# Retention layer: the prompt's inner products and state from rounded high and low parts, norm weights loaded head by head

## The reference, cut to what matters

```
def step(s, inp):
    qi, ki, vi = inp
    scores = jnp.einsum('bhik,bhjk->bhij', qi, ki) * decay_mat
    inner = jnp.einsum('bhij,bhjv->bhiv', scores, vi)
    cross = jnp.einsum('bhik,bhkv->bhiv', qi * q_decay, s)
    s_new = chunk_decay * s + jnp.einsum('bhjk,bhjv->bhkv', ki * k_decay, vi)
    return s_new, inner + cross
```

## Time and profile before

| what | value |
|---|---|
| time, median of 3 executions | 662.84 us (662.42 to 663.81) |
| the profiled execution, its span from first to last instruction | 663.5 us |
| what the page gives around the span | nothing; the slowest of the timed executions is 663.81 us |
| PE busy | 619.0 us, 93% of the span |
| DVE busy | 373.7 us, 56% |
| ACT busy | 231.5 us, 35% |
| POOL busy | 223.6 us, 34% |
| mean granted clock of PE | 0.978 |
| norm weights, one transfer | 1024 KB, 10.2 us to landing |

### The profile page before, as it was taken

The page is one execution under the profiler, slowest core; times in us unless marked ns, Lnnn a source line. Parts: engine busy times, 40 slices in busy tenths (PEclk is TensorE's granted clock), DMA queues, the critical chain, the costliest instruction groups (busy, mean ns, idle before and its releaser), DMA issues. The chain is left out here.

```text
span 663.5 us, 11322 instructions
## 1 busy us (share of the span) xinstructions
PE 619.0 (93%) x4307; PEld 383.2 (58%) x4307; DVE 373.7 (56%) x718; ACT 231.5 (35%) x475; POOL 223.6 (34%) x239
## 2 busy tenths in 40 slices
PE   6999999999999999998999999999999988659996
PEld 5676647664766476643467756677744555344441
DVE  3343847474747474726553733345797974783822
ACT  4255232623262326214142615555134246231010
POOL 0060218021802180214075248999910012020000
PEclk9899999999999999998999999999999999798998
DMA  8997376777687769794796563454999999999982
GB/s 297 379 389 283 127 254 218 285 289 254 221 302 271 251 215 325 257 382 186 279 329 233 200 203 126 146 194 131 392 368 406 410 408 405 410 399 409 401 349 87
DMA packets 82193, 190.28 MB, mean 287 GB/s; under 512 B 4119, under 2 KB 12583, under 8 KB 82012
## 3 DMA queue, kind: packets, MB, share of 16 engines
q1 hardware_dynamic: 80484, 183.70, 74.9%
q0 software_dynamic: 1120, 4.46, 1.9%
q10 hardware_dynamic: 536, 1.41, 0.6%
HBM read 167.14 MB, written 22.41 MB: 286 GB/s over the span
## 5 line engine op out<-in xcount | busy, mean ns | idle before, releaser
L533 POOL TENSOR_TENSOR weights_low<-ring,weights_high 128x512 fp32r<-128x512 f32 x96 | 123.9, 1330 | 81.4 <-PE bank L780 45.3
L1360 ACT ACTIVATE weights_high<-ring 128x1024 fp32r<-128x1024 f32 x84 | 86.6, 1055 | 103.7 <-PE bank L799 75.5
L791 PE MATMUL bank<-weights_high,h_high 128*128 128x512 f32 x272 | 109.2, 401 | 0.0
L791 PE MATMUL bank<-weights_high,h_low 128*128 128x512 f32 x272 | 106.9, 393 | 0.0
L799 PE MATMUL bank<-weights_low,h_high 128*128 128x512 f32 x272 | 82.5, 401 | 1.2 <-DVE weights_low L533 0.9
L791 PEld LDWEIGHTS bank<-weights_high,h_high 128*128 128x128 f32 x272 | 51.1, 188 | 25.5 <-issue 14.3
L533 DVE TENSOR_TENSOR weights_low<-ring,weights_high 128x512 fp32r<-128x512 f32 x72 | 44.8, 687 | 28.3 <-PE bank L780 16.9
L799 PEld LDWEIGHTS bank<-weights_low,h_high 128*128 128x128 f32 x272 | 49.9, 188 | 14.9 <-DVE weights_low L533 3.9
L791 PEld LDWEIGHTS bank<-weights_high,h_low 128*128 128x128 f32 x272 | 51.1, 188 | 11.1
L1675 POOL TENSOR_TENSOR keys_by_sequence<-key_parts,consts 128x2048 fp32r<-128x2048 f32 x4 | 15.1, 3764 | 111.0 <-DVE key_parts L1973 111.0
L1939 DVE SCALAR_TENSOR_TENSOR ring<-ring,bank 128x512 f32<-128x512 f32 x64 | 41.8, 685 | 17.8 <-PE bank L971 16.9
(11 more groups left out here) (257 smaller groups left out, 1011.8 us busy)
## 6 DMA issues: line engine op xcount, KB each, us to landing
ring<-in_w_ada SPq DMA_DIRECT2D x12, 2048.0 KB, 13.5
ring<-in_cache_k SPq DMA_DIRECT2D x40, 512.0 KB, 8.7
ring<-in_cache_v SPq DMA_DIRECT2D x40, 512.0 KB, 10.0
ring<-in_w_ret_in SPq DMA_DIRECT2D x8, 2048.0 KB, 11.4
ring<-in_state_ret SPq DMA_DIRECT2D x32, 512.0 KB, 9.5
out_state_sample<-ring SPq DMA_DIRECT2D x32, 512.0 KB, 6.1
ring<-in_w_moba_in SPq DMA_DIRECT2D x8, 2048.0 KB, 9.0
arena<-in_cache_k SPq DMA_DIRECT2D x24, 512.0 KB, 10.9
```

What stands on the lines that cost most here:

```text
L533: tensor_tensor(w_low[:, slot, k, :], ring[:, slot, k * CH:(k + 1) * CH], high[:, k, :].bitcast(F32), ALU.subtract).then_inc(low_ready[LOW ...
L791: pe.matmul(o[i][:, :], xs[p][i][:, k, :], high[:, k, :], start=k == 0 and p == 0, stop=False)
L1360: nc.scalar.activation(w_high[u[0] == "moba"][:, 2 * i:2 * i + 2, :].rearrange("p a b -> p (a b)"), w[:, 2 * i * CH:(2 * i + 2) * CH], ACT ...
```

## The change

The prompt's output rows and its state are no longer plain fp32 products. Values, decayed keys and decayed scores are split: ACT writes a rounded high part, DVE the low part, and PE adds three rounded products (high times high, low times high, high times low) for each plain one. One wait of PE is added, on `kd_ready`. `v_low`, `kd_low` and `s_low` take the places of `v`, `kd` and the scores; the high parts have places of their own. The norm weights are now loaded one head at a time by POOL, after the gate products of the head before, and POOL waits for them ahead of the gate products.

PE:

```
-                sealed(pe.matmul(o[:, :], L0["sT"][:, 0, :], v[:, 0, :], start=True, stop=True), ...)
+                def by_parts(o, pairs):
+                    terms = [(x, y) for high, low, v_n in pairs
+                             for x, y in ((high, v_high[:, v_n, :]), (low, v_high[:, v_n, :]), (high, v_low[:, v_n, :]))]
+                    for i, (x, y) in enumerate(terms):
+                        last = pe.matmul(o[:, :], x, y, start=i == 0, stop=i == len(terms) - 1)
+                    return last
+                sealed(by_parts(o, [(s_high[:, 0, :], s_low[:, 0, :], 0)]), ("row", "o", h, 0))
...
+                sealed(by_parts(o, [(s_high[:, 1, :], s_low[:, 1, :], 1), (s_high[:, 2, :], s_low[:, 2, :], 0)]),
+                       ("row", "o", h, 1))
...
-                        last = pe.matmul(o[:, :], kd[:, n, j * P:(j + 1) * P], v[:, n, :], start=n == 0, stop=n == 1)
+                    pe.wait_ge(kd_ready, 2 * h + 2)
+                    sealed(by_parts(o, [(kd_high[:, n, js], kd_low[:, n, js], n) for n in range(2)]), ("S", h, j))
```

ACT (the copy to `kd` now writes `kd_high`):

```
                 high_weights(("ret", h, 2), range(2, 4))
+                for n in range(2):
+                    o = wait_full(act, ("row", "ret", h, 1, n))
+                    nc.scalar.activation(v_high[:, n, :], o[:, :], ACT.Copy).then_inc(v_high_ready, 1)
                 if h:
                     for n in range(3):
                         turned(L0["yT"][:, 4 * h - 4:4 * h, :], ("yT", h - 1, n), n)
...
                 copy_part(("ada", 1, ADA_FIRST[h]))
+                act.wait_ge(s_plain_ready, h + 1)
+                nc.scalar.activation(s_high..., s_plain, ACT.Copy).then_inc(s_high_ready, 1)
```

DVE (the three value copies ahead of the `qkT` copies are gone; behind them now stands):

```
+                for n in range(2):
+                    wait_read(dve, ("row", "ret", h, 0, n))
+                    nc.vector.scalar_tensor_tensor(kd_low[:, n, :], L0["k"][:, n, :], const("kdec_n")...,
+                                                   kd_high[:, n, :].bitcast(F32), ALU.mult, ALU.subtract).then_inc(kd_ready, 1)
+                    o = wait_full(dve, ("row", "ret", h, 1, n))
+                    dve.wait_ge(v_high_ready, 2 * h + n + 1)
+                    read_out(nc.vector.tensor_tensor(v_low[:, n, :], o[:, :], v_high[:, n, :].bitcast(F32),
+                                                     ALU.subtract), label)
+                o = wait_full(dve, ("row", "ret", h, 1, 2))
+                read_out(nc.vector.tensor_copy(v[:, 2, :], o[:, :]), label)
                 low_weights(dve, nc.vector.tensor_tensor, ("ret", h, 2), ...)
...
+                wait_read(dve, ("scores", h))
+                dve.sem_inc(s_plain_ready, 1)
                 modulation_turned(1, ADA_FIRST[h])
+                dve.wait_ge(s_high_ready, h + 1)
+                nc.vector.tensor_tensor(s_low..., s_plain, s_high..., ALU.subtract).then_inc(sT_ready, 1)
```

POOL:

```
-            pool.dma_start(L0["gn"], t["ret_gn_g"].rearrange("o h v -> o (h v)").partition_broadcast(P)
-                           ).then_inc(gn_in, 16)
+            pool.dma_start(L0["gn"], t["ret_gn_g"][:, 0, :].partition_broadcast(P)).then_inc(gn_in, 16)
...
+                pool.wait_ge(gn_in, 16 * (h + 1))
                 for n in range(3):
                     ...
+                if h + 1 < RH:
+                    pool.wait_ge(gate_ready, 3 * h + 3)
+                    pool.dma_start(L0["gn"], t["ret_gn_g"][:, h + 1, :].partition_broadcast(P)).then_inc(gn_in, 16)
```

More of the change, by code:

```diff
@@ L81, in const_table @@
     put("kdec_0", gamma[None, :] ** (2 * P - 1.0 - i[:, None]) * DK ** -0.5)
+    put("kdec_n", np.concatenate([gamma[None, :] ** (n * P - 1.0 - i[:, None]) for n in (2, 1)], 1))
     put("cdec", gamma[None, :] ** (P - 1.0 - i[:, None]))
@@ L335, in build @@
                  ("qkT", (3, 4, P)), ("qpad", (2, NS * (32 + TS))),
-                 ("sT", (2, P)), ("sTc", (P,)), ("sTs", (32,)), ("S1", (2, DV)), ("yT", (RET_VT, ROWS)), ("gn", (RH * DV,))]
+                 ("sT", (2, P)), ("sTc", (P,)), ("sTs", (32,)), ("S1", (2, DV)), ("yT", (RET_VT, ROWS)), ("gn", (DV,)),
+                 ("vh", (2, DV)), ("kdh", (2, DK)), ("sTh", (3, P))]
         spec1 = [("slots", (2, KT * CH)), ("G", (3, D)), ("qbT", (MH * 4, 32)), ("qd", (2, D)), ("v", (3, D)),
@@ L369, in build @@
         vmix = rounded("value_parts", (DV,), in_arena(spec0, "vmix"))
+        v_high = rounded("v_high", (2, DV), in_arena(spec0, "vh"))
+        v_low = rounded("v_low", (2, DV), in_arena(spec0, "v"))
+        kd_high = rounded("kd_high", (2, DK), in_arena(spec0, "kdh"))
+        kd_low = rounded("kd_low", (2, DK), in_arena(spec0, "kd"))
+        s_high = rounded("scores_high", (3, P), in_arena(spec0, "sTh"))
+        s_low = rounded("scores_low", (3, P), in_arena(spec0, "sT"))
         h_high = rounded("h_high", (KT, ROWS), hT_at)
@@ L403, in build @@
             L1["slots"].rearrange("p a (j n) -> p (a j) n", j=4)]
+        s_at = in_arena(spec0, "sT") // 4 - arena_at // 4
+        s_plain = arena[:, s_at:s_at + 3 * P]
         last_part = L1["G"][:, 2, 0:CH]
@@ L448, in build @@
         state_new = sem("state_new")
+        v_high_ready, s_plain_ready, s_high_ready = (sem(n) for n in ("v_high_ready", "s_plain_ready", "s_high_ready"))
+        kd_ready = sem("kd_ready")
         state_out = [sem(f"state_out{i}") for i in range(2 * RH)]
@@ L960, in _ @@
             pe.wait_ge(sample_h, 1)
-            q, k, kd, v, qkT = (L0[x] for x in ("q", "k", "kd", "v", "qkT"))
+            q, k, v, qkT = (L0[x] for x in ("q", "k", "v", "qkT"))
             def new(h, s, j):
@@ L1037, in _ @@
                     o = open_bank(("S", h, j))
-                    for n in range(2):
-                        last = pe.matmul(o[:, :], kd[:, n, j * P:(j + 1) * P], v[:, n, :], start=n == 0, stop=n == 1)
-                    sealed(last, ("S", h, j))
+                    pe.wait_ge(kd_ready, 2 * h + 2)
+                    js = slice(j * P, (j + 1) * P)
+                    sealed(by_parts(o, [(kd_high[:, n, js], kd_low[:, n, js], n) for n in range(2)]), ("S", h, j))
             def last_head_turned():
@@ L1388, in _ @@
             high_weights(("ret", 0, 0), range(2, 4))
-            q, k, kd = L0["q"], L0["k"], L0["kd"]
+            q, k = L0["q"], L0["k"]
             for h in range(RH):
@@ L1407, in _ @@
                     if n < 2:
-                        nc.scalar.activation(kd[:, n, :], o[:, DK:2 * DK], ACT.Copy,
+                        nc.scalar.activation(kd_high[:, n, :], o[:, DK:2 * DK], ACT.Copy,
                                              scale=const(("kdec_0", "kdec_p")[n])[:, h:h + 1])
@@ L1427, in _ @@
                 copy_part(("ada", 1, ADA_FIRST[h]))
+                act.wait_ge(s_plain_ready, h + 1)
+                nc.scalar.activation(s_high[:, :, :].rearrange("p a b -> p (a b)"), s_plain, ACT.Copy).then_inc(s_high_ready, 1)
                 for layer, c in ADA_AT.get(h, ()):
@@ L1951, in _ @@
                             lambda k: k == 6 and part_left(("ret", h, 1)))
[L1952 to L1955, removed]
+                if h == 0:
+                    dve.wait_ge(tables_in, 16)
                 for n in range(3):
@@ L1966, in _ @@
                     read_out(ins, label)
+                for n in range(2):
+                    wait_read(dve, ("row", "ret", h, 0, n))
+                    nc.vector.scalar_tensor_tensor(kd_low[:, n, :], L0["k"][:, n, :],
+                                                   const("kdec_n")[:, RH * n + h:RH * n + h + 1],
+                                                   kd_high[:, n, :].bitcast(F32), ALU.mult, ALU.subtract).then_inc(kd_ready, 1)
+                    label = ("row", "ret", h, 1, n)
+                    o = wait_full(dve, label)
+                    dve.wait_ge(v_high_ready, 2 * h + n + 1)
+                    read_out(nc.vector.tensor_tensor(v_low[:, n, :], o[:, :], v_high[:, n, :].bitcast(F32),
+                                                     ALU.subtract), label)
+                label = ("row", "ret", h, 1, 2)
+                o = wait_full(dve, label)
+                read_out(nc.vector.tensor_copy(v[:, 2, :], o[:, :]), label)
                 low_weights(dve, nc.vector.tensor_tensor, ("ret", h, 2),
                             lambda k: k == 6 and part_left(("ret", h, 2)))
-                if h == 0:
-                    dve.wait_ge(tables_in, 16)
                 wait_read(dve, ("row", "ret", h, 0, 2))
```

15 lines of the change are left out of this document (6 added, 9 removed).

## The result

The changed kernel is slower. Its median is 665.97 us (663.73 to 668.28, six executions) against 662.53 us of the kernel before beside it; the ratio is 1.0052 with a 95% interval of 1.0033 to 1.0072. Measured once more, with the experiments, it was 664.74 against 662.89 us, ratio 1.0028 (1.0003 to 1.0052). Both say slower, by 2 to 3.5 us; for the second I had expected 3 to 3.5, and it gave 1.9. One execution takes up to 4 us more or less than the next, so single executions are compared stretch by stretch here and never by their whole time.

A forecast was written before the change was run, and what follows sets the result against it. PE was taken as full, with four points a head hanging closely on DVE or ACT. Terms -0.90 - 0 + 2.91 - 0.67 = +1.34 us gave 664.2 us, own range 663.3 to 665.2, outer range 662.3 to 666.4.

The forecast's parts named there:

- rival 4: Clock falls once more behind a widened wait: +1.7 us, 665.9 us; chance 0.10.
- PE's own work: Seven plain products a head become 21 rounded ones, 6.1 to 4.9 us: PE saves 1.25 us a head, 5.0 over four.
- Behind the state tiles: Heads 0 to 2: PE meets DVE's copies of the state tiles, keeps 0.30 of 1.25 us; 0.90 us gained.
- Behind head 3: PE's 1.97 us wait for the third norm's read takes in the saving, becoming 3.2 us; gain 0.
- ACT's two copies: Heads 1 to 3: value copies delay ACT's turned rows 0.97 us, PE's transpose wait becomes 1.35 us; 2.91 us lost.
- Head 0's transposes: DVE's value copies moved back, so its copy of the first transposed bank starts earlier; PE gains 0.67 us.
- Low weights: DVE's added work ahead of the gate projection's low weights fits with 0.4 us of slack; cost 0.
- Rival 3: Low weights late at the gate's projection, slack used up: +1.8 us on top, 666.0 us; chance 0.12.
- Samples' parts: DVE's samples' key and value parts shift 2.6 us, the second may meet POOL's gate products; cost 0, at most 0.2 a head.
- The scores' chain: DVE's scores, ACT's rounding, DVE's low part over by 154.5, wanted at 157.57 in head 1; cost 0, 3 us of cover.
- the clock: Half-speed PE clock for 3.4 us behind head 3's wait already costs 1.7 us; no further fall from wider transpose waits assumed.

The follow-up runs named there:

- new_late: Changed kernel with the samples' state products started two steps later in the next head's projection; 663.99 us, ratio 1.0019 to the kernel before.
- state_by_act: Changed kernel with ACT, not DVE, copying the two state tiles out of their banks; 661.32 us, ratio 0.9991 to the kernel before.
- turned_first: Changed kernel with ACT copying the turned rows first and rounding the values behind them; 662.57 us, ratio 0.9988 to the kernel before.
- before_act_copies: Kernel before with two unused ACT copies of 128x512 put ahead of the copies of the turned rows; 666.75 us, ratio 1.0055 to the kernel before.
- before_gn: Kernel before with only the norm weights loaded head by head, as in the change; 662.48 us, ratio 1.0008 to the kernel before.
- state_one: Changed kernel with only the product of the high parts in the prompt's state, 8 of 21 rounded products left out; 669.55 us, ratio 1.0103 to the kernel before.

## Why the prediction was right, and where it was not

The direction and the outer range (662.3 to 666.4) held; the size was under the measured one. The median of 665.97 us lies outside the forecast's own 663.3 to 665.2, next to the 665.9 of rival 4; the second one, 664.74, lies inside. "Slower" had about 0.48 against 0.40 for "no change", so that the direction was called by a hair, and some of its being right is luck.

- **PE's own work:** 1.25 us a head forecast, 1.16 measured (6.67 less 5.51).
- **Behind the state tiles:** 0.30 us a head kept was forecast, with 0.5 and 0.4 us at the two tiles; they measure 0.29 and 0.38. A head is 0.50 us longer, with 0.97 more at the transposes, so 0.47 is kept. My reason, that DVE's copies hang on the part ahead of the changed products, is right (8.04 against 8.15 us). That the bank of the state tiles decides was too narrow: new_late shows that DVE's work up to the samples' reads does, and state_by_act that 1.3 us less of it frees 0.7 us a head. The 0.17 us that I missed are partly the 0.11 us by which DVE's chain came nearer.
- **Behind head 3:** forecast 3.2 us of waiting, measured 3.10.
- **ACT's two copies:** forecast 1.35 us, measured 1.35, three times. turned_first and before_act_copies show the cause from both sides.
- **Head 0's transposes:** forecast a wait of 0.4 us in place of 1.10 and a gain of 0.67; the wait is 0.51 and the gain 0.6.
- **Low weights:** forecast slack 0.4 us, measured 0.5. Rival 3 did not come.
- **Samples' parts:** L2013, which was L1978, has 1677 ns as its shortest where it was 687: the second of the two instructions now meets POOL's gate products, as named, and PE did not wait for it.

```profile
L2013 DVE TENSOR_TENSOR value_parts<-arena,value_parts x8: 1677/2828/3977, 77.5 to 281.4; 32x512 fp32r<-32x512 f32 x8
```

- **The scores' chain:** its low part starts at 153.26 in head 1 and takes 0.56 us, PE waits for nothing there.

The sum of these was +1.34 us. In the profiles L702 starts 0.91 us later than L690 did while the retention layer's work began 0.5 us earlier, so +1.4 us; 0.5 us of that is the wait for the old state that I did not have, and the larger gain at the state tiles makes up for it. Up to there the steps hold.

The step that failed is **the clock, where I took none**. I put the fall in rival 4 with 0.10, and looked for it at the transposes, where 1.35 us of waiting let it stay. It was behind head 3, where I took the fall of the one profile that I had as given and assumed that it could not get worse: in the profile after it lasts 6.8 us and costs 2.7 us, where the 3.4 us cost 1.6 (21.01 less 19.37; I had priced them at 1.7). Five executions with the wait of 3.1 us left as it is had 6.8, 3.4, 3.4, 3.4 and 0 us of it at this place (the changed kernel twice, turned_first, new_late, state_by_act), and three with the wait of 1.97 us had 3.4, 0 and 0 us (before, before_gn, before_act_copies), so it is a matter of the execution, and seems likelier behind the longer wait; eight executions don't prove that, and state_one's three waits of 2.2 us each had one.

For the profiled pair the account closes. The stretch behind the wait is 1.1 us longer (22.15 against 21.01), which with the 1.4 us makes 2.5 us; the retention layer began 0.5 us earlier, and from these transposes to the end it was 335.6 in place of 336.2 us, which leaves the 1.5 us between the spans. That last part lasts between 333.8 and 336.9 us in the thirteen profiles here that can be read, whatever the kernel, and so makes much of the spread between executions. For the medians, 3.4 and 1.9 us, I can only estimate. The stretch behind the wait has a mean of 20.8 us in the five executions and 19.9 in the three, 0.9 us more; with the 1.4 us that is 2.3 us. How much of the rest is the clock and how much the spread stays open.

The 1.8 us around the span would have helped, had I known them: at 665.3 us the profiled execution of before was 2.5 us above its median, so that the fall in it need not be in a typical one.

## What to carry to other kernels

Fewer microseconds on the busiest engine are worth what the next engine's chain leaves: measure, from the trace, how far behind the shortened work the next bank, tile or read is ready, and subtract. Copies that are added for a cheaper product have to go behind what the busy engine waits for, in the queue of the engine that makes them; two instructions in the wrong order cost 0.97 us a head here, more than the 0.47 us that was kept of what 21 cheaper products had saved. When the saving turns into a longer wait, the clock can fall behind it, so either fill that wait with real work or shorten the chain that ends it; together these made the same products 5.7 us faster than the kernel before.

## What the runs showed of the hardware that I had not expected

- Leaving out 7.4 us of PE's work made the kernel 4.8 us slower (669.55 against 664.74 us), with the granted clock at 0.50 for 3.4 us behind waits of 2.2 us.
- The same wait of 3.1 us was followed by 6.8, 3.4 or 0 us at the lower level in different executions, one of 1.97 us by 3.4 or 0 us. The cost was half of the time in which PE was busy there: 2.7 us of 5.70, 1.3 of 2.80, 1.6 of 3.40.
- Products of 128x512 in plain fp32 have a pitch of 0.88 us, rounded ones 0.232 us, so three rounded ones are cheaper than a plain one by a fifth only: 0.70 against 0.88.
